# First attention: both components' score products issued as one alternating pair, behind the filler product

## The reference, cut to what matters

```python
s = jnp.einsum("bqhcd,bkhcd->bhcqk", q, k) * (ATT_QK_DIM ** -0.5)
p = jax.nn.softmax(s, axis=-1)
w = p[:, :, 0] - lam * p[:, :, 1]
return jnp.einsum("bhqk,bkhd->bqhd", w.astype(v.dtype), v)
```

## Time and profile before

| | |
|---|---|
| median of three executions | 2654.69 us (2652.11 to 2656.16) |
| profiled execution, span from first to last instruction | 2656.3 us |
| TensorE busy | 2499.0 us, 94% |
| VectorE busy | 1725.4 us, 65% |
| ScalarE busy | 960.6 us, 36% |
| mean granted TensorE clock over the span | 0.967 |
| TensorE busy from 225 to 300 us | 62.19 us of 75 |

### The profile page before, as it was taken

How to read it: one execution, slowest core, us unless ns; L and a number is a source line. 1 busy time by engine, 2 the same in 40 slices (tenths; PEclk the granted TensorE clock), 3 DMA queues, 4 the chain that set the end, 5 groups by cost and what they waited for, 6 DMA issues and landing times.

```text
span 2656.3 us, 26794 instructions
## 1 busy us (share of the span) xinstructions
PE 2499.0 (94%) x10562; PEld 1899.7 (72%) x10562; DVE 1725.4 (65%) x2192; ACT 960.6 (36%) x1262; POOL 103.3 (4%) x186
## 2 busy tenths in 40 slices
PE   6998769999994999999999999999999999999997
PEld 3884338788882788887774578888877646788886
DVE  7886588865658854668985585554689855733334
ACT  4324335422422422333554343222346543422221
POOL 0111000000000000000000000000000000000000
PEclk8998779999996999999999899999999998999999
DMA  7461002455552354553220124454522210223222
GB/s 279 154 229 40 16 16 103 150 173 179 168 175 86 111 187 168 168 175 127 80 90 23 39 103 159 159 187 158 177 95 86 78 36 30 82 91 107 96 87 80
DMA packets 66807, 315.25 MB, mean 119 GB/s; under 512 B 7128, under 2 KB 12632, under 8 KB 45817
## 3 DMA queue, kind: packets, MB, share of 16 engines
q1 hardware_dynamic: 41624, 222.29, 24.1%
q0 software_dynamic: 25056, 91.24, 10.5%
HBM read 311.40 MB, written 2.10 MB: 118 GB/s over the span
## 4 chain that ended last, share of the span: by engine, by line
PE 82%; DVE 13%; issue 1%; DMA 1%; ACT 1%; SPq 0%; DVEq 0%; ACTq 0%
PE psum L533 23%; PE psum L535 23%; PE psum L534 23%; PE psum L829 2%; DVE squares L1344 1%; PE psum L848 1%; DVE rstd L1296 1%; DVE x_lo L1339 1%; PE psum L858 1%; PE psum L847 1%; DVE w_lo L1445 1%; DMA big<-in_ada_first 1%; PE psum L880 1%; PE psum L666 1%; PE psum L725 1%
## 5 line engine op out<-in xcount | busy, mean ns | idle before, releaser
L533 PE MATMUL psum<-x_hi,w_hi 128*128 128x512 f32 x1968 | 782.5, 398 | 15.8 <-DVE squares L1394 10.7
L535 PE MATMUL psum<-x_hi,w_lo 128*128 128x512 f32 x1968 | 767.5, 390 | 0.0
L534 PE MATMUL psum<-x_lo,w_hi 128*128 128x512 f32 x1968 | 767.5, 390 | 0.0
L1445 DVE TENSOR_TENSOR w_lo<-w_raw,w_hi 128x2048 fp32r<-128x2048 f32 (+1 forms) x192 | 418.8, 2181 | 340.7 <-ACT w_hi L980 338.4
L980 ACT ACTIVATE w_hi<-w_raw 128x2048 fp32r<-128x2048 f32 (+1 forms) x192 | 350.5, 1825 | 528.7 <-DMA w_raw<-in_w 528.6
L533 PEld LDWEIGHTS psum<-x_hi,w_hi 128*128 128x128 f32 x1968 | 370.3, 188 | 110.5 <-issue 22.3
L534 PEld LDWEIGHTS psum<-x_lo,w_hi 128*128 128x128 f32 x1968 | 370.5, 188 | 78.9 <-issue 5.3
L535 PEld LDWEIGHTS psum<-x_hi,w_lo 128*128 128x128 f32 x1968 | 370.1, 188 | 78.3
L533 PE MATMUL psum<-hidden_hi,w_hi 128*128 128x512 f32 x912 | 356.4, 391 | 0.0
L535 PE MATMUL psum<-hidden_hi,w_lo 128*128 128x512 f32 x912 | 354.9, 389 | 0.0
L534 PE MATMUL psum<-hidden_lo,w_hi 128*128 128x512 f32 x912 | 354.8, 389 | 0.0
(11 more groups left out here) (389 smaller groups left out, 2544.6 us busy)
## 6 DMA issues: line engine op xcount, KB each, us to landing
w_raw<-in_w SPq DMA_DIRECT2D x160, 1024.0 KB, 4.9
ada_w<-in_ada POOLq DMA_DIRECT2D x164, 512.0 KB, 4.0
w_raw<-in_w SPq DMA_DIRECT2D x32, 704.0 KB, 4.1
big<-in_ada_first SPq DMA_DIRECT2D x12, 768.0 KB, 14.1
big<-in_ada POOLq DMA_DIRECT2D x10, 512.0 KB, 5.2
extra<-in_w_uq SPq DMA_DIRECT2D x8, 384.0 KB, 3.3
residual<-in_xT SPq DMA_DIRECT2D x2, 1024.0 KB, 9.6
cond_row<-in_c_row SPq DMA_DIRECT2D x4, 512.0 KB, 5.3
```

Of the source, the lines that this page charges most:

```text
L533: mm(o, w_h, x_h, start=first, stop=False)
L534: mm(o, w_h, x_l, start=False, stop=False)
L535: return mm(o, w_l, x_h, start=False, stop=last)
L1445: v.tensor_tensor(wl[:, r, 0:n], raw[:, r, 0:n], wh[:, r, 0:n].bitcast(f32), ALU.subtract).then_inc(w_split.sem, 1)
```

## The change

`scores1` loses its argument `parts`. It now waits once, for both exponentials of the step before, and then issues 512 keys of component 0, 512 keys of component 1, 256 keys of component 0, 256 keys of component 1. In the loops of all three engines filler A moves ahead of both components: TensorE issues A before the pair of scores, ScalarE copies A out before both exponentials, VectorE reads A (where it does) before both maxima. ScalarE waits for the end of its sine before it goes on. Sizes, buffers and banks stay as they are.

```diff
-            def scores1(n, parts=(0, 1)):
+            def scores1(n):
                 hd, q = steps1[n]
-                for c in parts:
-
-                    eng.wait_ge(S("exp1").sem, max(0, 2 * (n - 1) + c + 1))
-                    r = slice(64 * c, 64 * c + 64)
-                    mm(ps[:, 2 * c, :], big[r, hd, q * P:(q + 1) * P], KT1[r, hd, 0:T], start=True, stop=True)
-                    me.count(mm(ps[:, 2 * c + 1, 0:C], big[r, hd, q * P:(q + 1) * P],
-                                           KT1[r, hd, T:KEYS1], start=True, stop=True).then_inc(S("scores1").sem, 1), S("scores1"))
+                eng.wait_ge(S("exp1").sem, 2 * n)
+                for keys in (slice(0, T), slice(T, KEYS1)):
+                    for c in range(2):
+                        r = slice(64 * c, 64 * c + 64)
+                        ins = mm(ps[:, 2 * c + keys.start // T, 0:keys.stop - keys.start], big[r, hd, q * P:(q + 1) * P],
+                                 KT1[r, hd, keys], start=True, stop=True)
+                        if keys.start:
+                            me.count(ins.then_inc(S("scores1").sem, 1), S("scores1"))
...
             for n, (hd, q) in enumerate(steps1):
-                if n + 1 < len(steps1):
-                    scores1(n + 1, (0,))
...
                 fill(fill_of(n)[0])
                 if n + 1 < len(steps1):
-                    scores1(n + 1, (1,))
+                    scores1(n + 1)
...
-            def exps1(n, use=None):
+            def exps1(n):
                 for c in range(2):
-                    if c == 1:
-                        fill(use)
...
             for n, (hd, q) in enumerate(steps1):
+                fill(fill_of(n)[0])
                 if n + 1 < len(steps1):
-                    exps1(n + 1, fill_of(n)[0])
+                    exps1(n + 1)
...
             for n, (hd, q) in enumerate(steps1):
-                if n + 1 < len(steps1):
-                    max1(n + 1, (0,))
                 fill(fill_of(n)[0])
                 if n + 1 < len(steps1):
-                    max1(n + 1, (1,))
+                    max1(n + 1)
```

More of the change, by code:

```diff
@@ L1139, in sine @@
                 act((hidden1, hidden2)[n], ring_f[:, 2, 1, 0:256], ACT.Sin).then_inc(S("sines").sem, 1)
+                eng.wait_ge(S("sines").sem, n + 1)
             exps1(0)
```

## The result

| | before | after |
|---|---|---|
| median of this measurement | 2658.61 us (6 runs) | 2672.42 us (6 runs) |
| ratio | | 1.0058, 95% interval 1.0042 to 1.0074 |
| profiled execution, span | 2656.3 us | 2669.7 us |
| mean granted TensorE clock over the span | 0.967 | 0.964 |
| combination of step 1 to that of step 15 | 151.4 us | 165.8 us |

The changed kernel is 13.8 us slower by the medians (2672.42 - 2658.61) and 13.4 by the profiled spans. 2670.2 was forecast from a median of 2654.7, so 15.5 us of loss. (The kernel before was run again beside the changed one; its median moved up by 4 us.) The ratio is estimated over the executions with its interval and isn't the quotient of the two medians, which is 1.0052; its interval stands for a loss of 11 to 20 us.

The account below looks back on a forecast made before the run. The prediction saw no engine saturated in the attention, its steps running around a ring of engines. 2654.7 us, plus 8.5 for the longer ring at full clock, plus 7 for more half clock, gave 2670.2 us; range 2659 to 2678.

Parts of the forecast that it names:

- the ring: Attention round passing from engine to engine: filler A, component 1's scores, maximum, exponential, two copies, next filler A; 7.41 us before.
- A pair costs what one component costs; the alternation brings nothing: Attention scores on TensorE: both components together take 1.49 us, one alone 1.48; nothing counted for alternating.
- TensorE's relief: TensorE in 7 steps with a DFT filler as A: pairing frees some 1.49 us each, 10.4 us in all.
- The rival in which it pays: Rival: TensorE sets the attention's pace, so the freed 10.4 us come off, 2644.3 us; chance 0.05.
- The last link of the earlier trace: End of the old round: copy of filler B to next filler A, 0.93 us, put down to reading bank 7.
- The second maximum enters the ring, +1.0 a round: VectorE behind filler A: two maxima in a row, 1.95 us instead of 0.96; a round grows to 8.4 us.
- The table load enters behind a sine, +1.3: ScalarE in steps 0 and 2: exponential's table load waits for the first late maximum, before both exponentials; +1.3 us.
- +8.5 us at full clock: Attention's lateness up to step 15 without clock effects, going into the time in full; bounds 5 and 17 us.
- the bookkeeping: Three engines' attention programs laid side by side at full clock; 139.8 us from step 1 to 15 before, +8.5 after.
- +7 us by more half clock: TensorE in the attention: more idle stretches bring more time at 1.2 GHz; +7 us, bounds 0 and 12.
- The count of idle stretches: TensorE up to step 13: 13 stretches above 1.65 us instead of 7; six more at 1.66 us give +10.
- Lateness of each step: Combination's delay per attention step: +0.1 at step 1, 4.6 at 5, 6.6 at 7, 7.6 at 10, 8.5 from 13.

Follow-up runs that it names:

- e1: Changed kernel with the pair issued as component 0 whole, then component 1 whole; 2675.29 us, ratio 1.0068 to the kernel before.
- e2: Changed kernel with the alternating pair ahead of filler A, and A again between the components on ScalarE and VectorE; 2642.08 us, ratio 0.9941 to the kernel before.
- e3: Changed kernel with component 0's maximum over the first 128 of 768 scores; 2664.23 us, ratio 1.0023 to the kernel before.
- e6: Changed kernel with four idle products on TensorE behind filler B of steps 0 to 3; 2668.66 us, ratio 1.0051 to the kernel before.
- e5: Changed kernel with a single-column exponential behind each sine and the first three roots, loading the table early; 2668.58 us, ratio 1.0050 to the kernel before.
- e4: Kernel before with component 0's maximum over the first 128 of 768 scores; 2652.21 us, ratio 0.9979 to the unedited kernel before.
- e7: Changed kernel run again, unedited; 2673.36 us, ratio 1.0048 to the kernel before.
- e8: Changed kernel with three edits: component 0's short maximum, early exponential table load, idle products in steps 0 to 3; 2654.92 us, ratio 0.9981 to the kernel before.

## Why the prediction was right

Its mechanism held in the main: the change puts component 0's maximum and the table loads into the ring and brings more half clock. The total was off by 1.7 us (15.5 forecast, 13.8 measured); with an interval of 11 to 20 us, a match that close is in part luck. Step by step:

- *A pair costs what one component costs; the alternation brings nothing.* Right: 1.49 us in the profile after, and 1.50 in e1 without alternation. The Trainium skill ("TensorE: Matmul & The Clock Gate", Part 3) says that matmuls start and end in program order. The trace of e1 disagrees: by that rule the pair would have taken an estimated 2.4 us instead of 1.50.
- *TensorE's relief is worthless since TensorE isn't the bound.* Right in effect for this place: 11.5 us less busy and slower. The rival in which it pays (2644.3 us) was wrong about this kernel, but e2 shows that the relief is real once the waits are hidden: 2642.1 us, part of it by the clock.
- *The last link of the earlier trace rows, "since bank 7 must be read first", with component 0 nowhere in the ring.* This was misread. The copy of filler B ends at 335.59 (334.99 + 0.60), and in the changed kernel filler A follows such a copy within 0.05 us (258.72 + 0.60, then 259.37). What stands before filler A at 335.92 is component 0's scores:

```profile
334.43 1.12 PE L657 MATMUL psum<-big 64*128 64x512 f32 x2
...
335.40 0.59 PE L658 MATMUL psum<-big 64*128 64x256 f32 x2
```

  TensorE has no idle time in that round of the kernel before: filler A, a component, transposes, filler B and a component take 1.92 + 1.48 + 0.71 + 1.81 + 1.49 = 7.41 us. So TensorE did set the pace of this one round, and the ring of waits behind it was 7.13 us. Taking component 0 away could gain 0.28 us there, not 1.49, before the ring held the kernel; the direction of the forecast stands.
- *The second maximum enters the ring, +1.0 a round.* Right in kind: e3 took 0.67 us out of each first maximum and the rounds became shorter by that. In size it depends on what held the round before. The plain round at full clock took 8.15 us (step 4 to 5 in e6), 7.13 + 1.02, and that is 0.74 more than 7.41. The rounds of 8.4 us that the forecast wanted to see in the filter's steps are not there: step 11 to 12 and 12 to 13 took 10.9 and 10.8 us in the changed kernel, and 8.4 appears only in e5 (step 11 to 12).
- *The table load enters behind a sine, +1.3.* Right, twice 1.3 in e5, and in the round shown above. Behind the roots the combination of the same step doesn't feel it (step 7, where the prediction had counted part of it, and step 11). Behind the second root it delays the next filler A by 1.3 us, which the prediction did not have.
- *+8.5 us at full clock, 4.6 of it up to step 5.* Borne out in part. From step 1 to 5, e6 and e4 ran at full clock in the new and in the old order: 35.6 and 31.1 us, 4.5 apart, where the forecast has 4.6 - 0.1 = 4.5. (e4 has the shorter maximum, so the difference can be a little smaller.) For the later steps no run had a full clock throughout, so the other 3.9 us rest on the bookkeeping. (The upper end of the range takes 3 us for this part, where the bound of 17 would ask for 8.5; no measured number tests that.)
- *+7 us by more half clock.* The right kind, and over by 1 to 3: the changed kernel needs 165.8 us (164.1 in e7) where the bookkeeping has 148.3 at full clock (139.8 + 8.5), 17.5 us (15.8) for the half level against 11.6 before, so +5.9 (+4.2). This rests on the bookkeeping, and on one profile of the kernel before. The half-level time grew by 13.6 us, and a microsecond of it cost 0.32 us (17.5 / 54.6) against 0.28; from step 1 to 5, where runs at full clock give the measure, it was 0.30 to 0.35 (3.1 / 10.2, 4.8 / 13.7, 2.4 / 6.8). The count of idle stretches would have given +10. They often fell into stretches that were at the half level already (283 to 303 us is one), and not each of them brings the half level: the filler behind 2.57 us of idle time took 1.98 us, the full speed (249.94 in the round above).
- *Lateness of each step.* The total is right, the course is not. The loss from step 1 on was 6.9 us at step 5 (4.6 forecast without clock), 9.5 at step 7, but 8.3 at step 10 and 14.3 from step 13. Between 9 and 10 the changed kernel gained 2.2 us (14.9 against 17.1) where it should lose 1.0. The values product there ran partly at half clock before and at full clock after, 2.6 us less; first before, then after:

```profile
304.41 8.06 PE L666 MATMUL psum<-small,big 128*128 128x512 f32 x12
```

```profile
314.00 5.42 PE L667 MATMUL psum<-small,big 128*128 128x512 f32 x12
```

  Between 10 and 12 it then lost 6.6. Where a half-level stretch falls decides over single rounds; only the sum over many rounds could be forecast.

## What to carry to other kernels

When engines hand work round in a ring, freed time on one of them is worth something only if it was a link; what counts is what the edit moves into the ring. A piece of work between two users of one buffer (here the scores between fillers A and B of bank 7) is cover for the buffer's read: move it away, and the read, the wait and the clock that falls in the wait all come into the open. Keep the pairing, and put the pair where the single piece stood: e2 is the version to take, 0.6% faster than the kernel before. And compare single rounds only at the same granted clock: the unedited changed kernel took 11.1 us for step 1 to 2 in one execution and 9.4 in another.

## What the runs showed of the hardware that was not expected

- Idle products can hold the clock: 3.6 us of useless matmuls in each of four waits kept the granted clock at 1.00 instead of 0.87 (0.84 in e7) over 40 us, and four rounds became 4.8 us shorter (3.1 against e7). That the whole kernel gains by it is not shown (ratios 1.0051 against 1.0058 and 1.0048), and in e8, where the waits were shorter, they ran over.
- Products in different halves of the rows overlap whether they alternate or not (1.49 and 1.50 us for a pair whose halves take 1.48 each alone).
- ScalarE's table load can stand behind a wait that it doesn't need. It is placed with the first activation that wants the table, and waited for that activation's maximum (254.54 in the round above); one activation of a single column ahead of it took 1.3 us out of the ring. A load that a 3.35 us VectorE operation covers for the combination can still delay TensorE's next filler through ScalarE's copy.
- An idle stretch doesn't always bring the half clock: fillers and scores behind 2.57 us (changed kernel, 249.94) and 2.77 us (e2, 241.09) of idle time ran at full clock, while one behind 1.85 us before was slowed to 2.97 us.
